# Probabilities of the FoX and band heads laid out by key block, split with the values into high and low parts, and one TensorE product per key block in three passes

## What is computed

```python
s = jnp.einsum('bqhd,bkhd->bhqk', qi, k).astype(jnp.float32) * scale
s = s + ci.transpose(0, 2, 1)[..., None] - ct[:, :, None, :]
s = jnp.where(kpos[None, :] <= qpos[:, None], s, NEG_INF)
p = jax.nn.softmax(s, -1).astype(v.dtype)
return jnp.einsum('bhqk,bkhd->bqhd', p, v)
```

## Time and profile before

| what | value |
|---|---|
| median of 3 runs | 2008.84 us (2008.29 to 2010.16) |
| time of the profiled execution | 2006.87 us |
| its span | 2005.3 us |
| TensorE busy | 97% |
| VectorE busy | 66% |
| ScalarE busy | 39% |
| mean granted TensorE clock | 0.989 |

### The profile page before, as it was taken

The page is one execution under the profiler, slowest core; times in us unless marked ns, Lnnn a source line. Parts: engine busy times, 40 slices in busy tenths (PEclk is TensorE's granted clock), DMA queues, the critical chain, the costliest instruction groups (busy, mean ns, idle before and its releaser), DMA issues.

```text
span 2005.3 us, 37656 instructions
## 1 busy us (share of the span) xinstructions
PE 1941.4 (97%) x15484; PEld 1913.9 (95%) x15484; DVE 1322.8 (66%) x2233; ACT 788.2 (39%) x1311; POOL 192.9 (10%) x300
## 2 busy tenths in 40 slices
PE   7979999999999999999997999999999999999995
PEld 6869999999999999999997999999999999999995
DVE  6976666666565445687887767677665535557777
ACT  6433333333233233544573433343332322344444
POOL 0311110000100000000003111000001000000000
PEclk9989999999999999999999999999999999999998
DMA  7533333322522122555663333322234222325563
GB/s 296 187 134 114 115 115 112 107 96 91 182 73 98 69 91 81 196 202 195 222 207 109 115 115 115 112 99 92 101 119 158 80 92 68 106 75 208 185 224 130
DMA packets 66691, 265.02 MB, mean 132 GB/s; under 512 B 10812, under 2 KB 20668, under 8 KB 50640
## 3 DMA queue, kind: packets, MB, share of 16 engines
q1 hardware_dynamic: 40112, 202.13, 29.1%
q0 software_dynamic: 16000, 46.54, 6.6%
q10 hardware_dynamic: 10432, 14.29, 2.0%
HBM read 233.37 MB, written 32.16 MB: 132 GB/s over the span
## 4 chain that ended last, share of the span: by engine, by line
PE 90%; DVE 5%; DMA 2%; issue 1%; ACT 1%; SPq 0%; ACTq 0%; DVEq 0%
PE GB L643 34%; PE GB L530 24%; PE GB L554 19%; PE AB L583 3%; PE AB L625 3%; PE GB L858 2%; DMA WR<-in_wt 2%; PE AB L594 2%; DVE WL L1447 1%; DVE WL L1312 1%; PE AB L630 0%; DVE XL L1680 0%; PE AB L610 0%; PE AB L633 0%; DVE TLOW L1492 0%
## 5 line engine op out<-in xcount | busy, mean ns | idle before, releaser
L643 PE MATMUL GB<-XH,WH 128*128 128x272 f32 x1392 | 408.6, 294 | 22.3 <-DVE WL L1447 19.0
L643 PE MATMUL GB<-XH,WL 128*128 128x272 f32 x1392 | 403.9, 290 | 0.0
L643 PE MATMUL GB<-XL,WH 128*128 128x272 f32 x1392 | 403.3, 290 | 0.0
L917 ACT CAST WH<-WR 128x2048 fp32r<-128x2048 f32 x120 | 229.0, 1908 | 425.3 <-PE GB L530 222.0
L1312 DVE TENSOR_TENSOR WL<-WR,WH 128x2048 fp32r<-128x2048 f32 x120 | 274.9, 2291 | 156.9 <-ACT WH L917 143.6
L976 ACT CAST WH<-WR 128x512 fp32r<-128x512 f32 (+1 forms) x224 | 165.3, 743 | 326.9 <-PE GB L643 165.9
L643 PEld LDWEIGHTS GB<-XH,WH 128*128 128x128 f32 x1392 | 264.9, 190 | 24.8 <-DVE WL L1447 19.8
L643 PEld LDWEIGHTS GB<-XH,WL 128*128 128x128 f32 x1392 | 264.9, 190 | 0.0
L643 PEld LDWEIGHTS GB<-XL,WH 128*128 128x128 f32 x1392 | 264.2, 190 | 0.0
L1447 DVE TENSOR_TENSOR WL<-WR,WH 128x512 fp32r<-128x512 f32 (+1 forms) x224 | 195.4, 875 | 23.9 <-ACT WH L976 22.4
L530 PE MATMUL GB<-XH,WH 128*128 128x272 f32 x1280 | 176.4, 290 | 0.0
(11 more groups left out here) (249 smaller groups left out, 3010.7 us busy)
## 6 DMA issues: line engine op xcount, KB each, us to landing
WR<-in_wt SPq DMA_DIRECT2D x120, 1024.0 KB, 4.8
WR<-in_wt SPq DMA_DIRECT2D x128, 512.0 KB, 4.4
XR<-out POOLq DMA_DIRECT2D x64, 136.0 KB, 2.8
out<-OY ACTq DMA_DIRECT2D x24, 272.0 KB, 2.2
out<-OY ACTq DMA_DIRECT2D x8, 544.0 KB, 5.1
out<-KT POOLq DMA_DIRECT2D x16, 272.0 KB, 3.6
out<-VT POOLq DMA_DIRECT2D x16, 272.0 KB, 3.5
o_rest<-OS POOLq DMA_DIRECT2D x16, 272.0 KB, 2.3
```

What stands on the lines that cost most here:

```text
L643: mm = pe.matmul(out, w[:, k, :], x[:, k, :], start=(start and k == 0 and i == 0), stop=(stop and k == chunks - 1 and i == 2))
L917: act.copy(WH[:, s, :, :], WR[:, s, :, :]).then_inc(hi, 1)
```

## The change

For the FoX and band heads alone:

- `turn_probs` writes the ten transposed blocks in the order of `key_order`: the four blocks that use key block 0 into bank 0, three with key block 1 (and one with key block 3) into bank 1, two with key block 2 into bank 2. It is the same ten transposes.
- ScalarE copies the three banks to `PTH` as fp32r (`probs_hi`), and the values to `VH` as fp32r (`take_v_hi`) where `take_v` stood.
- VectorE subtracts (`probs_lo`): `PTL` from banks 0 to 2, two small copies to `PT`, the sample values, and a new `VL`.
- `mix` multiplies the prompt part in three passes (VH by PTH, VL by PTH, VH by PTL), each of four matmuls of 512, 384, 256 and 128 columns, in place of ten float32 matmuls of 128 columns.
- `turn_v` waits for all three counts of `pte`, that is until VectorE has read banks 0 to 2 and the small blocks. `mix` also waits for `v_low`.
- The new tensors lie over old ones (VH over V, PTL over S, PTH over PT, VL over BI).

```diff
+        key_order = [(i, 0) for i in range(4)] + [(i, 1) for i in range(1, 4)] + [(3, 3), (2, 2), (3, 2)]
+        key_cols = [(0, 0, 4), (1, 4, 3), (2, 8, 2), (3, 7, 1)]
...
-                j = 0
-                for i in range(4):
-                    for b, kb in enumerate(g.blocks[i]):
-                        mm = pe.matmul(AB[:, 3, P * i:P * (i + 1)], V[:, kb, :], pt_col(j),
-                                       start=(b == 0), stop=(b == len(g.blocks[i]) - 1))
-                        j += 1
+                if g in (FOX, BAND):
+                    pe.wait_ge(v_low, vu_low + 1)
+                    for p, (v, t) in enumerate(((VH, PTH), (VL, PTH), (VH, PTL))):
+                        for kb, j, n in reversed(key_cols) if p == 2 else key_cols:
+                            mm = pe.matmul(AB[:, 3, P * kb:], v[:, kb, :], t[:, P * j:P * (j + n)],
+                                           start=(p == 0 and kb == 0), stop=(p == 2 and kb == 0))
...
                 def all_values():
                     pe.wait_ge(c_out, taken(b, "c12"))
+                    pe.wait_ge(pte, 3 * u + 3)
                     turn_v()
...
+            def probs_hi(u, i):
+
+                for b in range(3):
+                    if b < 2:
+                        act.wait_ge(pt, 3 * u + b + 1)
+                    else:
+                        act.wait_ge(p_turned, i + 1)
+                    w = P * (4 if b < 2 else 2)
+                    act.copy(PTH[:, 512 * b:512 * b + w], AB[:, b, 0:w]).then_inc(p_high, 1)
...
                 if last:
+                    probs_hi(u, l * 2 * GH + i)
                     act.wait_ge(b_pe, ran(b, "p3"))
                     w_hi(l * LT + C0, 0, l * (LT // 2) + C0 // 2 + 1)
                 else:
-                    for name in ("a11", "d1", "a12"):
+                    for name in ("a11", "d1"):
                         block_hi(b + 1, name)
+                    probs_hi(u, l * 2 * GH + i)
+                    block_hi(b + 1, "a12")
                     block_hi(b + 1, "d2")
-                take_v(vu)
+                take_v_hi(vu)
...
+            def probs_lo(u, i, vu):
+
+                dve.wait_ge(p_turned, i + 1)
+                for b in range(3):
+                    w = P * (4 if b < 2 else 2)
+                    dve.wait_ge(p_high, 3 * i + b + 1)
+                    low = dve.tensor_tensor(PTL[:, 512 * b:512 * b + w], AB[:, b, 0:w],
+                                            PTH[:, 512 * b:512 * b + w].bitcast(F32), ALU.subtract)
+                    if b < 2:
+                        low.then_inc(pte, 1)
+                dve.tensor_copy(PT[:, 10 * P:10 * P + 2 * DEC], AB[:, 2, 256:256 + 2 * DEC])
+                dve.tensor_copy(PT[0:DEC, 10 * P + 2 * DEC:PTW], AB[0:DEC, 2, 320:320 + DEC]).then_inc(pte, 1)
+                dve.wait_ge(pt, 3 * u + 3)
+                dve.tensor_copy(V[0:DEC, 4, :], AB[0:DEC, 2, 352:352 + P]).then_inc(vse, 1)
+                dve.wait_ge(ve, vu + 1)
+                dve.tensor_tensor(VL[:, :, :], AB[:, 3, :].rearrange("p (b d) -> p b d", b=4), VH[:, :, :].bitcast(F32), ALU.subtract) \
+                    .then_inc(v_low, 1)
```

More of the change, by code:

```diff
@@ L220, in encoder_step @@
         GA = sb("GA", [P, TOK])
+        VH = sb_at("VH", [P, 4, HD], top[0], F32R)
         V = sb("V", [P, NT, HD])
+        PTL = sb_at("PTL", [P, 10 * P], top[0], F32R)
         S = sb("S", [P, SW])
+        PTH = sb_at("PTH", [P, 10 * P], top[0], F32R)
         PT = sb("PT", [P, PTW])
@@ L225, in encoder_step @@
         VC = sb("VC", [P, 2, HD])
+        VL = sb_at("VL", [P, 4, HD], top[0], F32R)
         BI = sb("BI", [P, SEQ + PAST + DEC])
@@ L372, in encoder_step @@
         c_out = sem("c_out")
+        p_turned = sem("p_turned")
+        p_high = sem("p_high")
+        v_low = sem("v_low")
         x_sums = sem("x_sums")
@@ L591, in turn_probs @@
                 blocks = [(i, b) for i in range(4) for b in range(len(g.blocks[i]))]
+                if g in (FOX, BAND):
+                    blocks = key_order
                 for j, (i, b) in enumerate(blocks):
@@ L611, in turn_v, with mix @@
                 mm.then_inc(vt, 1)
-            def mix(g, u, kl, vu=None, dm=None):
+            def mix(g, u, kl, vu=None, dm=None, vu_low=None):
                 pe.wait_ge(pte, 3 * u + 3)
@@ L621, in mix @@
                     pe.wait_ge(ld_vm, 16 * (dm + 1))
-                j = 0
-                for i in range(4):
-                    for b, kb in enumerate(g.blocks[i]):
-                        mm = pe.matmul(AB[:, 3, P * i:P * (i + 1)], V[:, kb, :], pt_col(j),
-                                       start=(b == 0), stop=(b == len(g.blocks[i]) - 1))
-                        j += 1
+                if g in (FOX, BAND):
+                    pe.wait_ge(v_low, vu_low + 1)
[4 more added lines that the diff above has]
+                else:
+                    j = 0
+                    for i in range(4):
+                        for b, kb in enumerate(g.blocks[i]):
+                            mm = pe.matmul(AB[:, 3, P * i:P * (i + 1)], V[:, kb, :], pt_col(j),
+                                           start=(b == 0), stop=(b == len(g.blocks[i]) - 1))
+                            j += 1
                 mm.then_inc(pv, 1)
@@ L724, in all_probs @@
                 def all_probs():
-                    turn_probs(g, u)
+                    turn_probs(g, u).then_inc(p_turned, 1)
                 def all_values():
                     pe.wait_ge(c_out, taken(b, "c12"))
+                    pe.wait_ge(pte, 3 * u + 3)
                     turn_v()
@@ L732, in head @@
                 two_tiles(l, b, all_scores, all_probs, all_values)
-                mix(g, u, kl, vu)
+                mix(g, u, kl, vu, vu_low=l * 2 * GH + i)
             def pair(n, m, u, kl, vu, dm, last):
@@ L931, in exps, with take_v_hi @@
                                    accum_out=esum[0:r, i:i + 1]).then_inc(ex, 1)
+            def probs_hi(u, i):
+                for b in range(3):
+                    if b < 2:
+                        act.wait_ge(pt, 3 * u + b + 1)
+                    else:
+                        act.wait_ge(p_turned, i + 1)
+                    w = P * (4 if b < 2 else 2)
+                    act.copy(PTH[:, 512 * b:512 * b + w], AB[:, b, 0:w]).then_inc(p_high, 1)
+            def take_v_hi(vu):
+                act.wait_ge(vt, vu + 1)
+                act.copy(VH[:, :, :], AB[:, 3, :].rearrange("p (b d) -> p b d", b=4)).then_inc(ve, 1)
             def take_v(vu):
@@ L1552, in head @@
                     block_lo(b + 1, "a12")
-                take_probs(g, u, vu)
+                probs_lo(u, l * 2 * GH + i, vu)
                 take_product(b, "c21", GA[:, half(0)])
```

## The result

| | median | runs | ratio to before, 95% interval |
|---|---|---|---|
| before | 2008.74 us | 4 | |
| after | 2023.12 us (2021.87 to 2023.70) | 4 | 1.007 (1.0052 to 1.0087) |

The kernel before has one run more here than in the table ahead of the prediction, so its median is 2008.74 and not 2008.84. The change costs 14.4 us by the medians, 10.4 to 17.5 by the interval; 13.5 were forecast.

A forecast was written before the change was run, and what follows sets the result against it. TensorE's stream, busy 97%, was taken to bound the kernel. Ordinary heads 5.3, last heads 6.5 and clock 1.7 gave +13.5 us on the median 2008.84: 2022.3 us, range 2015.0 to 2030.0.

The forecast's parts named there:

- values' transposes late, ordinary head: In 14 heads, TensorE waits for VectorE's reads of banks 0 to 2, delayed by the a12 cast: 0.57 us late.
- product's start, late: Ordinary heads: wait for VL about nil, but another weight load exposed, so the product starts 0.69 us late.
- product: Probabilities times values: twelve fp32r matmuls take 1.92 us as in the scores, against 2.23, saving 0.31 a head.
- net of an ordinary head: Late product start less the product's saving: +0.38 us in each of 14 heads, +5.3 us together.
- wait in a last head: Last head of each layer: 128x2048 cast and subtraction delay the values' transposes 3.46 us; net +3.27, twice +6.5.
- falls of the clock: TensorE's clock halves after a long last-head wait; one fall in two layers, +1.7 us, ends 0 and 3.4.
- sum: Whole kernel: ordinary heads 5.3, last heads 6.5 and clock 1.7 make +13.5 us.
- other pitches than in the scores: Sign of a wrong prediction: the product's twelve matmuls spaced differently in time from the same shapes in the scores.
- Faster: Rival: both waits stay hidden, only the product's saving of 16 x 0.31 = 5.0 us remains: 2003.8 us; chance 0.05.
- only the last heads pay: Rival: ordinary heads gain 0.2 to 0.31 us each, the last heads still cost 6.5: 2012.9 us; chance 0.07.
- The product is no cheaper: Rival: fp32r with few columns costs as much as float32, 5.0 us more: 2027.3 us; chance 0.08.
- The delay spreads: Rival: VectorE reaches the next head's blocks late, TensorE waits for WL, another 0.5 us a head: 2030.3; chance 0.06.

The follow-up runs named there:

- experiment 4: Changed kernel with a12 cast before PTH, PTL before the last heads' 128x2048 subtraction, VL awaited only before the third pass, product in bank 0: 2003.66 us.
- experiment 3: Changed kernel with passes reordered, VL waited for only ahead of the third, and the product in PSUM bank 0: 2022.42 us.
- experiment 1: Changed kernel with ScalarE's a12 cast put back ahead of the PTH copies in the 14 ordinary heads: 2021.69 us.
- experiment 6: Changed kernel with one more 512-column VectorE subtraction ahead of PTL in each of the 16 heads: 2035.03 us.
- experiment 7: Changed kernel with the product done as ten float32 matmuls of VH and PTH, all splits and waits kept: 2030.68 us.
- experiment 2: Changed kernel with PTL and the small copies ahead of VectorE's 128x2048 subtraction in the two last heads: 2015.94 us.
- experiment 5: Changed kernel without making PTL and VL; all three passes multiply VH by PTH, so the result lacks low parts: 2008.02 us.

## Why the prediction was right

**Step by step.** The place of each term held, and its size nearly:

| step | predicted | measured |
|---|---|---|
| values' transposes late, ordinary head | 0.57 us | 0.56 |
| product's start, late | 0.69 us | 0.56 + 0.14 = 0.70 |
| product | 1.92 us | 1.98 |
| net of an ordinary head | +0.38 us | +0.46 |
| wait in a last head | 3.46 us | 3.44 |
| falls of the clock | one, 1.7 us | one and two in two profiles, some 1.3 us each |
| sum | +13.5 us | +14.4 (medians) |

The ordinary heads make 14 x 0.46 = 6.4 us. The last ones make 3.44 each, less the 0.25 us that the product saves, and 0.14 us of the second wait where the clock holds: some 3.3, 6.6 for both. With one fall of the clock that is 14.3 us, near the 14.4 of the medians. The closeness is in part luck: the interval leaves room for 10.4 to 17.5, the number of falls changes from run to run, and the later load above isn't in this sum. The forecast's own errors also cancel in part, 1.1 us too little for the ordinary heads and 0.4 too much for the clock.

**The product's size was off.** The same twelve shapes took 1.92 us in the scores, and in experiment 4, but 1.98 in the change: behind a wait the first matmul holds the engine 0.30 us from its start to the next one's, where in experiments 3 and 4, without the wait, it is 0.24. I counted the exposed weight load into the start and left the product at 1.92; that is 0.06 us a head. The forecast had named other pitches than in the scores as a sign of being wrong. For this one matmul the sign came, and the term it stands in is 0.06 us off; the other eleven, in another order than in the scores, take 1.67 us together, where the scores' take 1.68. That the second weight load makes it is likely (it starts late as well) but not shown by an experiment.

**The clock term was sized too high and its frequency too low.** I took 1.7 us for a fall and one fall in two layers. What one costs can be read in the two last heads of the first profile: from the values' transposes to the product it is 533.73 - 530.20 = 3.53 us with the fall, 1517.20 - 1515.00 = 2.20 without, so 1.3. It is less than half of 3.4 because the fall's first 0.2 us lies over idle time, and because VL is there when the slower TensorE comes to the product, so that the second wait doesn't show. A second reading is layer 1 from head 0's values' transposes to those of the first pair: 1564.94 - 1139.27 = 425.67 us in the first profile, without a fall, and 1567.07 - 1140.00 = 427.07 in the second, with one, 1.4 apart. Of the twelve waits of 3.3 to 3.9 us ahead of the last heads' transposes, in the two profiles of the changed kernel and those of experiments 1, 3, 6 and 7, eleven were followed by a fall. The Trainium skill, "TensorE: Matmul & The Clock Gate", section "HAM oscillation — how this bites in real kernels", has long waits of TensorE throttle it and the next burst start cold. Eleven of these twelve waits agree, and the one in layer 1 of the first profile doesn't; I had counted on one of two.

**The rivals.** "Faster" and "only the last heads pay" fell with the sixteen rows of L619. "The product is no cheaper" fell with experiments 4 and 7. "The delay spreads" fell with the distance of 53.27: no wait but the two showed in the heads. What I said against "faster" was the a12 cast's place, and experiments 1 to 4 show just this: with the cast and the last heads' subtraction moved and VL's wait put off, the rival's 2003.8 us is what experiment 4 measures (2003.66).

**What stays open.** The 2 us by which the two profiled spans differ beyond the medians stand at the layers' starts: head 0 of layer 0 is reached 1.2 us later (1.1 of it the load above), and from layer 0's pairs to head 0 of layer 1 it is 1.1 us longer. The second is within what the kernel before does by itself: that stretch is 415.1, 415.2 and 417.5 us in its three profiles, 416.7 and 416.5 in the two of the changed kernel. The first recurs in all profiles of changed kernels but experiment 7's, and may be part of the change's cost, with the cause open. Why one wait of the twelve had no fall behind it is open too.

## What to carry to other kernels

A split into high and low parts costs little by amount where two engines have idle time (experiment 4 makes all parts, and its heads don't wait for them), but each part is a new link in a chain across engines, and its price is the place in each engine's stream. Ask which older instruction stands ahead of the new link and whether it is needed sooner: here a cast that only the next head's products read, more than 9 us later (254.00 against 263.46), stood behind the copies, and its subtraction ahead of the new ones. And when a wait is taken away, work out the next one before the experiment; in experiment 1 some 0.4 of 0.56 us went on to the next wait.

## What was not expected of the hardware

- A new wait of TensorE of 3.3 to 3.9 us in the last heads was followed by half clock, mostly for 3.4 us, in 11 of 12 cases; one of 1.75 us (experiment 5, both layers) was not. The stretch behind it in layer 0, clock third from the end:

```profile
523.60:527.00 3.40, 3.33 (x26) 3.28 (x26) 0.72 (x2) 1.18 (x2) 0.00 (x0) 1.00 0.74 243
```

- A matmul of 512 columns that is first behind a wait holds TensorE 0.30 us and not 0.24; that is seen with VL's wait and gone without it (experiments 3 and 4).
- A median over four runs of kernels with this clock fall moves by 1 to 2 us between kernels for reasons that the heads' distances don't show, so an effect of 0.1 us in each of 16 heads is better read from the timeline than from the time.
